# Token stage, scan and combination of a hybrid flow kernel: rolled loop with bodies of four tiles in place of two

## What is computed

```python
z = h @ lp['w_in']
y_rwkv, s_final = rwkv7_bidirectional(...)
x = x + ga1 * mix
x = x + ga2 * routed_moe(h, router_w, router_b, ...)
```

## Time and profile before

| | |
|---|---|
| median of three executions | 3972.12 us (3970.88 to 3974.76) |
| the profiled execution | 3966.32 us, its span 3964.5 us |
| granted TensorE clock, mean | 0.949 |
| TensorE matmul busy | 3638.9 us (92%) |
| TensorE weight loads busy | 2884.9 us (73%) |
| VectorE busy | 1398.0 us (35%) |
| GpSimd busy | 1046.8 us (26%) |
| ScalarE busy | 785.9 us (20%) |

### The profile page before, as it was taken

The page is one execution under the profiler, slowest core; times in us unless marked ns, Lnnn a source line. Parts: engine busy times, 40 slices in busy tenths (PEclk is TensorE's granted clock), DMA queues, the critical chain, the costliest instruction groups (busy, mean ns, idle before and its releaser), DMA issues. The chain is left out here.

```text
span 3964.5 us, 64158 instructions
## 1 busy us (share of the span) xinstructions
PE 3638.9 (92%) x24967; PEld 2884.9 (73%) x24968; DVE 1398.0 (35%) x2878; ACT 785.9 (20%) x1467; POOL 1046.8 (26%) x1506
## 2 busy tenths in 40 slices
PE   8999999996899999999799999999999949999960
PEld 4676666674798999999789989989989934444420
DVE  2444444443645444444121222222222242222227
ACT  1222222222333333332011111111111101111113
POOL 0333333332455555554011011011011000000013
PEclk9999999997899999999899999999999969999985
DMA  8323222324332333331711011011011144765236
GB/s 291 107 101 104 92 92 88 105 96 147 97 102 67 90 100 102 102 102 36 270 45 65 35 41 65 35 41 65 35 44 61 43 165 165 259 226 187 90 107 216
DMA packets 296969, 424.33 MB, mean 107 GB/s; under 512 B 122415, under 2 KB 205997, under 8 KB 296749
## 3 DMA queue, kind: packets, MB, share of 16 engines
q1 hardware_dynamic: 259244, 349.55, 26.4%
q0 software_dynamic: 11952, 43.52, 3.3%
q10 hardware_dynamic: 25552, 27.93, 2.0%
HBM read 287.99 MB, written 132.94 MB: 106 GB/s over the span
## 5 line engine op out<-in xcount | busy, mean ns | idle before, releaser
L1808 PE MATMUL c_ps<-c_hT,big 128*128 128x128 f32 x6528 | 752.7, 276 | 25.1 <-DMA big<-in_w_in 25.1
L1808 PEld LDWEIGHTS c_ps<-c_hT,big 128*128 128x128 f32 x6528 | 743.9, 193 | 33.0 <-issue 29.3
L695 PE MATMUL a_ps<-front,a_hT 128*128 128x512 f32 (+1 forms) x1088 | 416.1, 540 | 3.5 <-DVE a_mix L597 3.5
L2231 PE MATMUL e_ps<-big,e_xT 128*128 x784 | 347.5, 596 | 2.3 <-DVE e_xT L2193 2.3
L695 PEld LDWEIGHTS a_ps<-front,a_hT 128*128 128x128 f32 x1088 | 204.0, 190 | 199.5 <-issue 187.0
L689 PE MATMUL a_ps<-a_hT,front 128*128 128x128 f32 x2992 | 344.7, 277 | 2.3 <-ACT a_hT L360 2.3
L689 PEld LDWEIGHTS a_ps<-a_hT,front 128*128 128x128 f32 x2992 | 341.4, 193 | 6.2 <-issue 2.9
L2231 PEld LDWEIGHTS e_ps<-big,e_xT 128*128 128x128 f32 x784 | 149.4, 191 | 191.7 <-issue 191.7
L918 POOL TENSOR_TENSOR b_tmp<-b_tt,b_ta 128x126 f32<-128x126 f32 (+22 forms) x496 | 191.2, 386 | 246.4 <-DMA b_ta<-s_a 208.8
L1808 PE MATMUL c_ps<-c_wo,c_mT 128*128 128x512 f32 x544 | 236.3, 592 | 0.0
L1773 DVE TENSOR_TENSOR c_gs<-c_gs,c_ps 128x384 f32<-128x384 f32 x136 | 75.4, 554 | 445.0 <-PE c_ps L1808 434.7
(11 more groups left out here) (317 smaller groups left out, 5093.7 us busy)
## 6 DMA issues: line engine op xcount, KB each, us to landing
big<-in_exp_w SPq DMA_DIRECT2D x48, 1024.0 KB, 10.2
s_D<-a_shared SPq DMA_DIRECT2D x34, 768.0 KB, 6.0
front<-s_D SPq DMA_DIRECT2D x34, 768.0 KB, 7.3
s_yr<-e_yo ACTq DMA_DIRECT2D x49, 512.0 KB, 3.0
front<-s_A SPq DMA_DIRECT2D x34, 512.0 KB, 5.9
a_aw<-in_ada_w SPq DMA_DIRECT2D x32, 512.0 KB, 6.6
s_A<-a_shared SPq DMA_DIRECT2D x17, 768.0 KB, 3.4
big<-in_w_in SPq DMA_DIRECT2D x12, 1024.0 KB, 12.2
```

The costliest lines, as they stand in the source:

```text
L695: ins = nc.tensor.matmul(ps[:, bank, 0:width], hT[b][:, k, :], win[:, k, c:c + width], start=k == 0, stop=k == KD - 1)
L1808: return nc.tensor.matmul(out, lhsT, rhs, start=start, stop=stop)
L2231: return nc.tensor.matmul(out, lhsT, rhs, start=start, stop=stop)
```

## The change

The rounds of `over_tiles` go from six with a body of two tiles to three with a body of four. The body is written out by a Python loop: `i` runs from 2 to 5, so the tile is `j * 4 + i`, the buffer `i % 2` and the use count `j * 2 + i // 2`, for `j` = 0, 1, 2. That is again tiles 2 to 13, in the same order, with the same buffers and the same waits. The straight tiles at both ends are untouched. All five engines of the token stage and of the scan go through it, and SyncE, ScalarE and VectorE of the combination. Merge and experts have loops of their own.

```diff
     for t in range(2):
         step(t, t, 0, 3)
-    with e.Fori(1, LAT // 2 - 1) as j:
-        step(j * 2, 0, j, 3)
-        step(j * 2 + 1, 1, j, 3)
+    with e.Fori(0, LAT // 4 - 1) as j:
+        for i in range(2, 6):
+            step(j * 4 + i, i % 2, j * 2 + i // 2, 3)
     for t in range(LAT - 2, NT):
         step(t, t % 2, t // 2, LAT - t)
```

## The result

The changed kernel takes 4000.75 us, the median of six executions (3976.76 to 4007.06), against 3972.03 us before on the same chip (3970.08 to 3974.76). The ratio is 1.0059 with a 95% interval of 1.0031 to 1.0087. On another chip, twelve executions gave 3987.55 us against 3970.50 us, ratio 1.0040 (1.0018 to 1.0061). So it is slower by 0.4 to 0.6%. I had forecast 6 us faster, and 3954 to 3981 us as the range.

The account below looks back on a forecast made before the run. It took TensorE and its granted clock as the bound, a loop's end mattering only where it stops TensorE. Scan branches -10.7, slow stretches -4.9, token branches +9.4 gave -6.2 us: 3972.1 to 3966 us, range 3954 to 3981.

Parts of the forecast that it names:

- The branches: Token stage: two taken TensorE branches go from 0.2 to about 3.7 us, 4.7 us lost each with the clock, 9.4 together.
- The literal two-page window: Skill's fetch rule, taken literally: the token body would miss already and the change only drop branches; the forecast rejected it.
- The scan's branches: Scan: three of five taken branches go, at 3.6 us each, a gain of 10.7 us; bounds 5.6 and 12.3.
- The slow stretches: Scan tiles 1 to 14: one of six mid-tile 1.2 GHz stretches goes, 4.9 us gained; bounds 14.6 gained, 4.9 lost.
- The dear token branch: Token stops bring 13.65 us at 1.2 GHz each, 18.8 us in all; scan returns only 5.6; +13.2 us, 3985; chance 0.15.
- The harmless branch: Token stage: longer body's branch costs nothing, store being larger or wait hidden; -15.6 us, 3956 us; chance 0.20.
- slow stretches stay six: Scan: the count of mid-tile half-clock stretches doesn't change; -1.3 us in all, 3971 us; chance 0.20.
- The covers I named for VectorE and GpSimd: Any 3.9 us branch could hide behind VectorE's 6.08 us wait for ScalarE at L497 and GpSimd's 12.15 us at L1161.
- A price of the combination: Combination: its path runs through gathers issued by unchanged GpSimd code; forecast zero, within half a microsecond.
- The sign that I had named: Combination: a change of over a microsecond there would show the forecast wrong.

Follow-up runs that it names:

- the tokens' experiment: Bodies of four tiles in the token stage alone, scan and combination with two, against the kernel before: 3975.69 us against 3964.13, ratio 1.0025.
- the second profile: The changed kernel once more, unaltered, against the kernel before on another chip: 3987.55 us against 3970.50, ratio 1.0040.
- the changed kernel with the moves: Changed kernel, VectorE masking AqkT before transposing diagonal blocks, SyncE issuing next scan loads before waiting for diagonal blocks: 3934.43 us, 5.7 above two-tile loops so reordered.
- the three scans with both moves: Kernels with VectorE's AqkT masks and SyncE's next scan loads issued earlier: two-tile loops 3928.70 us, scan without a loop 3918.75, bodies of four 3934.43.

## Why the prediction was wrong

**The branches: right.** A body of 2,198 matmuls and weight loads doesn't fit, and the token branch takes 3.8 us (forecast 3.7), with instruction packets now fetched in every round, 19 between 300 and 700 us where before there were none. The stops are 2.99 and 2.93 us (forecast 2.9). The price with the clock was 7.8 us in the first profile and 4.7 in the second, for a term of 9.4. The Trainium skill's 2,048 instructions of store ("Runtime: NRT & Kernel Launch", Instruction fetch mechanics) agree with the traces of both stages: bodies of 1,099 are quick, of 2,065 and 2,198 slow. The literal two-page window doesn't, by the 0.208 us at 1,099.

**The scan's branches: somewhat over-sized.** Three at 3.6 us were to give 10.7 us. Over a slow tile's 55.02 us, the five cost 17.8 us before and the two that are left 8.6, in both profiles of the changed kernel: 9.2 us back. I took the price from rounds in which the clock fell behind the stop. Where it doesn't, as in the scan of the tokens' experiment, one is worth 2.1 us, three 6.3.

**The slow stretches: the step that failed.** I wrote that the alternation of long and short tiles was due to the two-tile round and that, broken up, it would leave one slow tile fewer, with one more as the bound. The first half was right and the conclusion had the wrong sign. The round wasn't what made every second tile slow, it was what kept every other one quiet. Instead of -4.9 us the step was +24.5 us in the first profile and +14.7 in the second (6 against 11 and 9 slow tiles). The spans of the first pair are 38.5 us apart, and the traces account for it by tiles, each counted from its first product with `Shd`: tokens +7.8; the way into tile 0 -1.1; tile 0, slow after and not before, +4.9; tiles 1 to 14 +18.8, which is 24.4 for five slow tiles, less 9.2 for three branches, and 3.6 for two falls of 13.65 in place of 10.24 us and small rests; tile 15 +11.2; tile 16 and the end of the scan -4.9; all between the scan and the combination +0.7; the combination and the end +1.1. So tiles 0 and 15, which my forecast left out, add nearly as much as tiles 1 to 14, and by falls of the clock too. In the second profile tiles 1 to 14 are 7.4 us longer than before and tile 15 is 11.2 us longer.

The rows had held the evidence. Every tile behind a scan branch had the full clock, five of five; of the seven others in the rounds five hadn't. I counted tiles 1, 2, 12 and 13 as a sign that straight code is quiet; tile 12 lies behind a branch.

**The rivals.** The dear token branch came nearest in time (3985 us) but not in mechanism: it asked 18.8 us of the token stops, and they cost 7.8 and 4.7. The half of it that said that the scan's pauses pull the clock down elsewhere pointed the right way, but stopped at giving back less, where the scan lost. The harmless branch was wrong, and "slow stretches stay six" wrong on the low side. The covers I named for VectorE and GpSimd weren't needed. A price of the combination isn't shown: the stretch from L2407 to L2394 took 112.5 to 115.5 us in the nine profiles with two-tile bodies, and 114.1, 114.5, 116.6 and 116.9 us in the four with bodies of four. The sign that I had named, a change of over a microsecond, was finer than that spread.

**What stays open.** That a stop keeps the next tile quiet is shown by the stops put in by hand. Why it does, and which of the other tiles turn slow, isn't. A likely way is timing. In the scan without a loop a slow tile lasts 55.0 us and falls in successive tiles start 54.6 us apart, so each comes 0.4 us earlier in its tile: 1.7, 1.3 and 0.9 us behind the first product with `Shd`, then a quiet tile, then 1.5, 1.1 and 0.7, again a quiet tile. Whether the clock falls would then hang on the moment of the pause, and a stop would act by moving it. That is argued, not tested: no run shifts the pause without a stop. Nor are pauses the only thing ahead of a fall: in tile 15 of the changed kernel the second one, of 13.65 us, has no pause over 0.5 us in the 10 us ahead of it, and tile 15 of the changed kernel with the moves shows the same. Nor is it shown why the first six executions of before agree within 5 us and later ones on other chips spread over 48 us.

## What to carry to other kernels

In this kernel a rolled loop's end costs nothing while the body fits TensorE's instruction store, and a longer body can push it out; compare the branch's duration per stage before changing the body. Where TensorE is nearly always busy, a pause of 1.1 to 2 us can be followed by 10.24 us at half clock, another 4.9 us; it isn't each time, and once 0.85 us was enough. Look for the pause and its cause, here the order of two operations on VectorE and of two loads on SyncE, before touching the loop. When one pause goes, check the trace for the wait that takes its place, and leave a stop that shields the tile behind it where it is until the pauses are gone. Count the slow tiles in more than one profile: the same two-tile scan had 3, 6 and 8.

## What the hardware showed unexpectedly

Idle time can pay: five stops of 3.15 us took the count of slow tiles from 10 to 5, and the kernel wasn't slower than before (1.0004, 0.9984 to 1.0023). The clock fell after pauses of 1.1, 1.34 and 1.7 us, but not after each, and only once for 10 us in tiles 1 to 14 of the three scans with both moves, where the pauses inside a tile were mostly 0.5 to 0.7 us and at most 1.3 us. The second instruction queue (q14) went from 34 packets to 62 without a single branch over 0.075 us on VectorE in either stage, and between 300 and 700 us, inside the token rounds, it moved 13 packets where it had moved none. So the doubled bodies of the other engines were fetched again without a visible wait.
